# Running sums of the forget logs placed between inner steps of the query projection's second pass

## The reference

```python
z = rms_norm(h, g_mix) @ w_in          # q_a, k_a, v_a, q_b, k_b, v_b, f_b, gates
log_f = jax.nn.log_sigmoid(f_logit)    # (B, S, 8 heads)
c = jnp.cumsum(log_f, axis=1)          # running sums over the tokens
s = einsum(q, k) * scale + c[query] - c[key]
```

## Time and profile before

| | us |
|---|---|
| median of 3 runs | 1789.91 |
| profiled execution, its own time | 1788.2 |
| span of the profiled execution | 1786.4 |
| PE busy | 1738.9 (97% of the span) |
| DVE busy | 1121.7 (63%) |
| ACT busy | 700.6 (39%) |

### The profile page before, as it was taken

How to read it: one execution, slowest core, us unless ns; L and a number is a source line. 1 busy time by engine, 2 the same in 40 slices (tenths; PEclk the granted TensorE clock), 3 DMA queues, 4 the chain that set the end, 5 groups by cost and what they waited for, 6 DMA issues and landing times.

```text
span 1786.4 us, 21129 instructions
## 1 busy us (share of the span) xinstructions
PE 1738.9 (97%) x8437; PEld 1461.0 (82%) x8437; DVE 1121.7 (63%) x1425; ACT 700.6 (39%) x1089; POOL 268.1 (15%) x350
## 2 busy tenths in 40 slices
PE   7999999999899999999999999999999999999998
PEld 7887877887898788887888888888887788888886
DVE  5652565543996876589848866974887256445423
ACT  5332465652896331553233323323344244233212
POOL 2000021211785225100000000000002132000101
PEclk9999999999999999999999999999999999999999
DMA  5777977687661772283272255227211112211222
GB/s 179 264 261 277 326 248 244 236 328 189 131 143 60 254 277 105 84 288 135 71 288 100 84 212 212 95 94 282 71 48 36 59 60 101 65 54 41 78 112 94
DMA packets 137811, 280.69 MB, mean 157 GB/s; under 512 B 9520, under 2 KB 29552, under 8 KB 134256
## 3 DMA queue, kind: packets, MB, share of 16 engines
q1 hardware_dynamic: 137712, 279.33, 46.1%
HBM read 212.16 MB, written 67.14 MB: 156 GB/s over the span
## 4 chain that ended last, share of the span: by engine, by line
PE 82%; DVE 7%; ACT 3%; DMA 2%; issue 2%; POOL 2%; SPq 1%; POOLq 0%; ACTq 0%; DVEq 0%
PE PS L710 13%; PE PS L711 13%; PE PS L712 13%; PE PS L955 10%; PE PS L956 10%; PE PS L957 10%; PE PS L686 3%; PE PS L847 2%; PE PS L849 2%; PE PS L848 2%; DVE WB L1871 1%; POOL TF L2156 1%; DMA RAW<-in_w_br_swa 1%; PE PS L869 1%; PE PS L814 1%
## 5 line engine op out<-in xcount | busy, mean ns | idle before, releaser
L1061 ACT ACTIVATE WH<-WB 128x2048 fp32r<-128x2048 f32 x56 | 107.3, 1916 | 295.1 <-PE PS L957 239.7
L710 PE MATMUL PS<-UH,RHL 128*128 128x512 f32 (+1 forms) x512 | 191.5, 374 | 4.3 <-DVE UL L1476 2.4
L1476 DVE TENSOR_TENSOR WB<-WB,WH 128x2048 fp32r<-128x2048 f32 x56 | 128.2, 2289 | 99.7 <-ACT WH L1061 99.7
L712 PE MATMUL PS<-UH,RHL 128*128 128x512 f32 (+1 forms) x512 | 190.1, 371 | 0.0
L711 PE MATMUL PS<-UL,RHL 128*128 128x512 f32 (+1 forms) x512 | 190.0, 371 | 0.0
L955 PE MATMUL PS<-WH,AH 128*128 128x512 f32 x448 | 175.1, 391 | 4.0 <-DVE H L1832 2.3
L955 PE MATMUL PS<-AH,WH 128*128 128x512 f32 x448 | 174.6, 390 | 0.0
L956 PE MATMUL PS<-WB,AH 128*128 128x512 f32 x448 | 174.4, 389 | 0.0
L957 PE MATMUL PS<-WH,AL 128*128 128x512 f32 x448 | 174.4, 389 | 0.0
L957 PE MATMUL PS<-AH,WB 128*128 128x512 f32 x448 | 174.3, 389 | 0.0
L956 PE MATMUL PS<-AL,WH 128*128 128x512 f32 x448 | 174.3, 389 | 0.0
(11 more groups left out here) (256 smaller groups left out, 3807.5 us busy)
## 6 DMA issues: line engine op xcount, KB each, us to landing
WB<-in_w_ff SPq DMA_DIRECT2D x32, 1024.0 KB, 9.2
AH<-uf_scratch SPq DMA_DIRECT2D x21, 1024.0 KB, 5.3
AL<-uf_scratch SPq DMA_DIRECT2D x21, 1024.0 KB, 7.4
GX<-gates_scratch SPq DMA_DIRECT2D x64, 256.0 KB, 3.5
gates_scratch<-GST SPq DMA_DIRECT2D x56, 256.0 KB, 4.2
H<-in_x SPq DMA_DIRECT2D x16, 512.0 KB, 8.7
RAW<-in_w_in SPq DMA_DIRECT2D x16, 512.0 KB, 6.9
UH<-ugT_scratch SPq DMA_DIRECT2D x8, 1024.0 KB, 7.1
```

Source lines behind the costliest of these rows:

```text
L710: pe.matmul(o_ap, sh, mh, start=first, stop=False)
L712: ins = pe.matmul(o_ap, sl, mh, start=False, stop=last)
L1061: return act.activation(dst, src, ACT.Copy, **more)
L1476: return dve.tensor_tensor(dst, src, high.bitcast(F32), ALU.subtract)
```

## The change

The 8 products of the running sums and the transpose leave their place between the two projections. They become two functions, which `products` calls in the second query pass: `sum_logs` after the matmuls of step k = 3, `turn_logs` after those of step k = 5. On ScalarE the negated copy, and on VectorE the copy to C, move ahead of the four spills of the second query pass, and so stand right behind the T1 block's halves. SyncE's order is untouched.

```diff
-            def projected(name, slab):
+            def projected(name, slab, between=None):
...
                     products([by_columns(slab, j, h, b, spill_sum, (name, j, h), u_is("mix", 7)) for (j, h), b in zip(gr, bs)],
-                             range(8), [slab] if j0 else ())
-
-            projected("qb", S_qb)
-            take(0, *c_copied.of())
-            on.wait_ge(*log_dve.of("done"))
-            LF = FT[:, 5, :]
-            pe.matmul(PS[:, 0, 0:64], tri, LF, start=True, stop=False)
-            for j in range(1, NT):
-                ins = pe.matmul(PS[:, 0, 8 * j:64], ones, LF[:, 0:64 - 8 * j], start=False, stop=(j == NT - 1))
-            ins.then_inc(*c_sum.up())
-            take(1, *c_negated.of())
-            on.wait_ge(*c_copied.of())
-            pe.transpose(PS[0:64, 1, 0:P], C, ident).then_inc(*c_turned.up())
+                             range(8), [slab] if j0 else (), between if j0 else None)
+
+            def sum_logs():
+                take(0, *c_copied.of())
+                on.wait_ge(*log_dve.of("done"))
+                LF = FT[:, 5, :]
+                pe.matmul(PS[:, 0, 0:64], tri, LF, start=True, stop=False)
+                for j in range(1, NT):
+                    ins = pe.matmul(PS[:, 0, 8 * j:64], ones, LF[:, 0:64 - 8 * j], start=False, stop=(j == NT - 1))
+                ins.then_inc(*c_sum.up())
+
+            def turn_logs():
+                take(1, *c_negated.of())
+                on.wait_ge(*c_copied.of())
+                pe.transpose(PS[0:64, 1, 0:P], C, ident).then_inc(*c_turned.up())
+
+            projected("qb", S_qb, {3: sum_logs, 5: turn_logs})
             projected("kb", S_kb)
...
             turned_high("T1")
-            projected("qb", 1)
             on.wait_ge(*c_turned.of())
             copy(CT[0:64, :], PS[0:64, 1, 0:P], scale=-1.0).then_inc(*c_negated.up())
+            projected("qb", 1)
             turned_high("T4")
...
             turned_low("T1")
-            projected("qb", 1)
             on.wait_ge(*c_sum.of())
             dve.tensor_copy(C, PS[:, 0, 0:64]).then_inc(*c_copied.up())
+            projected("qb", 1)
             turned_low("T4")
```

## The result

The changed kernel takes 1791.14 us (median of 22 runs, 1787.87 to 1795.38), the kernel before beside it 1788.63 (22 runs). The ratio is 1.0012, 95% interval [1.0007, 1.0018]: +2.1 us (+1.3 to +3.2). It is slower, by less than the 0.2% that was taken as the bound. The profiled execution took 1792.15 us, its span is 1790.3. That is 3.9 us more than the span before: 1.1 us lie ahead of the change, 2.3 at its place, and about 0.5 behind it. The forecast was +2.6 us. The forecast time of 1792.5 us was counted from 1789.91, the median of 3 runs; the 22 runs beside the changed kernel put the kernel before 1.3 us lower.

What follows compares the result with a forecast made beforehand. PE, busy 97% of the span, was taken as the bound. New cost 1.8 + 5.8 + 0.3 + 2.66 = 10.6 us against 7.98 gave +2.6 us, so 1792.5 us; range 1788 to 1796.5.

Steps and rivals of the forecast that it cites:

- The chain that holds the place: Transpose waits for transfer, ScalarE's split, T1's high half, T1's low half and VectorE's copy to C; it starts at 138.25.
- Sums: The 16 running-sum matmuls on PE after step 3 of the second query pass, claimed to cost 1.8 us.
- idle: PE's wait before the transpose after step 5, claimed to be 5.8 us where it was 2.71.
- the step from the transpose to the next matmul: On PE, time until step 6 begins after the transpose; between 0.11 and 0.41 us, taken as 0.3.
- clock: Loss to PE's slow clock after the gap at the transpose, taken as 2.66 us, bounds 1.6 to 3.4.
- The negated copy: PE's 0.36 us wait for ScalarE's negated copy before the kb pass, claimed to cost nothing after the change.
- The stores that come later: SyncE's GR fetches and stores go out some 8 us later; with 14 us free, none was to reach PE.
- The later waits: PE waits after 150 were to stay; one gone or new by more than 1 us would show the forecast wrong.
- The count of slow matmuls: Slow matmuls after a PE start vary between runs, 6, 11 or 14; estimated loss 1.2 to 2.9 us here.
- Rival C: The new gap before the transpose leaves PE's clock untouched: -0.1 us, 1790 us; chance 0.12.
- Rival B: Copy to C is ready when PE reaches the transpose at 132.4, leaving no gap: -5.9 us, 1784 us; chance 0.08.

Runs made afterwards that it cites:

- e2: Changed kernel with VectorE's copy to C moved ahead of the last two kb loads' low parts and T1's low half; -4.1 us against the kernel before.
- e7: Changed kernel with T1's halves and the copy to C ahead of the splits of the last two kb loads; -5.4 us against the kernel before.
- e1: Changed kernel with the transpose after step 7 of the second query pass instead of step 5; -4.7 us against the kernel before.
- e5: Changed kernel with the transpose after step 6 instead of step 5; -0.4 us (-2.0 to +1.3) against the kernel before.
- e3: Changed kernel's ScalarE and VectorE copies alone, with PE's sums and transpose between the projections as before; -3.9 us against the kernel before.
- e4: Changed kernel with 22 more matmuls filling PE's wait before the transpose; +2.3 us (+0.7 to +3.8) against the kernel before.
- e9: The changed kernel run again, with nothing altered; +1.3 us (-0.5 to +3.2) against the kernel before.
- e12: The kernel before, unchanged, profiled a second time; +0.1 us to the gates in its trace, timed in one run only.
- e6: Changed kernel with the sums after step 1 instead of step 3; +1.6 us (0 to +3.2) against the kernel before.

## Why the prediction was right, point by point

**The chain that holds the place.** Right, and shown: the copy's place (e2), T1's place behind the transfer (e7), the transpose's place (e1, e5) each take the wait away or shorten it, and the transpose of e1, e3, e4 and the changed kernel lies 23.9 to 24.1 us after the pass's start whatever PE does ahead of it.

**The sizes.** Sums 1.8 us said, 1.7 measured; idle 5.8 said, 5.78 measured from the end of step 5; the step from the transpose to the next matmul 0.3 said, 0.05 measured; clock 2.66 said, 2.58 and 1.74 measured in two executions. The whole: +2.6 said, +2.3 and +1.5 to the gates, +2.1 timed. The hit on the clock is partly luck: executions of the same program lose 1.7 to 2.6 us there, and with 1.74 the sum would have been 0.9 us lower.

**The negated copy.** Said to cost nothing, and it does in the changed kernel. That it costs 0.36 us without its cover was seen in e1 and e3.

**The stores that come later.** SyncE's GR fetches and spill stores did move, from 24.5 to 32.3 us after the pass's start, as this row of the changed kernel tells:

```profile
147.66 0.93 SPq L2288 DMA_DIRECT2D GR<-in_w_in  x2
```

In the traces nothing of it reached PE: from the gates to the feed-forward's first matmul the changed kernel takes 558.5 us (e9 557.5), the kernel before 558.1 and 559.1. No run moves these transfers alone, so that they cost nothing in the times is argued, not shown.

**The later waits.** "A PE wait after 150 new by more than 1 us" was named as a sign of being wrong, and it is there. One wait of 3.7 us ahead of 452.3 was 2.4 us before, but e12, the kernel before itself, has it at 3.7 as well. One of 1.17 us ahead of 624.3 is in neither trace of the kernel before and is 0.6 us in e9; its cause stays open. Both lie in the stretch that takes as long as before, so neither enters the sum.

**The count of slow matmuls.** The Trainium skill (TensorE: Matmul & The Clock Gate, section "What's actually happening") says the number of slow matmuls after a start varies from run to run of one kernel. The traces agree, for a fall in mid-kernel: 13 and 8 slow spacings in two executions of the changed kernel. The kernel before had 13 in both of its own.

**Rival C.** That the new gap doesn't touch the clock is refuted: both executions of the changed kernel fell to 1.2 GHz in it.

**Rival B.** Its price was right (-5.9 us; -6.0 to the gates in e2 and e7, -4.1 and -5.4 timed), and its condition was too: the copy has to be there when PE comes. In the changed kernel it isn't. What I had as B's only way, a shorter transfer, was too narrow: the order of VectorE does it.

**What was off.** I read the earlier trace rows as saying that the transfer's end follows from its issue. e6 contradicts that. It didn't enter the sum, because the change doesn't move that issue. The step from the transpose to the next matmul was taken 0.25 us too long.

## What to carry to other kernels

Before work is moved into a gap or a running pass, follow what it waits for back through the other engines' own orders: the two parts here made PE ask 5.8 us ahead of VectorE's answer. Moving the answer (the copies) alone gained 3.9 us; asking earlier as well pays only once the answer is early too (6.0 us to the gates in e2 and e7, against 4.9 for the copies alone; the times, 4.1 and 5.4 against 3.9, don't tell them apart). And a PE wait of 2 to 3 us is to be priced at up to twice its length: where the clock fell in one, the slow matmuls behind it cost 1.4 to 2.7 us more, but it didn't fall in each.

## What the runs showed of the hardware

The clock fell in the waits of 5.6, 3.3, 2.7 and 2.2 us above, not in those of 0.8 us and less. In between the length of the wait doesn't decide. At the place of the earlier trace rows it fell in waits of 2.23 us (before) and 2.30 us (e12), and stayed at 1.00 in 2.31 us (e5) and in 2.47 us (the changed kernel):

```profile
590.25 0.47 PE L710 MATMUL PS<-OBH,RHL 128*128 128x512 f32 x1 [2.47 <-DVE Y L1790]
```

After it had fallen the loss was 1.4 to 2.7 us, and it wasn't larger behind the longer waits. What the loss does follow is how long PE works after the wait before the full clock is back: 5.4 us in the changed kernel, 3.6 in e9 and 2.8 in e5, with 2.58, 1.74 and 1.37 us lost.

A transfer issued 1.8 us later landed at the same time (e6), in a stretch with four spill stores and another fetch issued ahead of it. That the transfers ahead set its end is my reading; no run tested it. The traces fit it: in the changed kernel and in e6 the fetch issued ahead took 8.4 us, this one landed 1.3 us after it, and the mean busy share of the 16 DMA engines was 1.00 to 1.01 from 120 to 132.
